# The order of the two token halves in the low-part product of a split float32 projection

## The reference

```python
for i in range(DEPTH):                       # DEPTH = 4
    a = rms_norm(h, norm_mix[i])
    # i % 3 == 0: stick-breaking attention: qkv = a @ w_qkv (1024 x 3072), ..., o @ w_o (1024 x 1024)
    # i % 3 == 1: short gated convolution:  a @ w_in (1024 x 3072), ..., (gate_b * y) @ w_out
    # i % 3 == 2: gated linear attention:   a @ w_in (1024 x 3088), ..., (o * silu(g_out)) @ w_o
    h = h + mixer(a)
    a = rms_norm(h, norm_mlp[i])
    h = h + (relu(a @ w_up) ** 2) @ w_down   # 1024 x 4096 and 4096 x 1024
y = rms_norm(h, norm_final)
```

## Time and profile before

| | |
|---|---|
| median of three runs | 2761.11 us |
| profiled execution, its own time | 2760.71 us |
| its span, first to last instruction | 2759.0 us |
| TensorE busy (matmul) | 2729.8 us, 99% of the span, 20754 matmuls |
| VectorE busy | 1266.0 us, 46% |
| ScalarE busy | 864.6 us, 31% |
| mean busy share of the DMA engines, GB/s | about 2 tenths, 81 GB/s |
| mean granted TensorE clock | 0.995 of full speed |

### The profile page before, as it was taken

The page is one execution under the profiler, slowest core; times in us unless marked ns, Lnnn a source line. Parts: engine busy times, 40 slices in busy tenths (PEclk is TensorE's granted clock), DMA queues, the critical chain, the costliest instruction groups (busy, mean ns, idle before and its releaser), DMA issues.

```text
span 2759.0 us, 48416 instructions
## 1 busy us (share of the span) xinstructions
PE 2729.8 (99%) x20754; PEld 2657.8 (96%) x20754; DVE 1266.0 (46%) x1577; ACT 864.6 (31%) x949; POOL 223.1 (8%) x232
## 2 busy tenths in 40 slices
PE   8999999999999999999999999999999999999998
PEld 8987999999999999999999899999999969999998
DVE  4258433333455434334478543333342494433433
ACT  3147322222312322223224432222331384321222
POOL 4000100000211100000133110000010001000001
PEclk9999999999999999999999999999999999999999
DMA  4211322222222222222212122222222103322221
GB/s 158 78 66 37 115 82 85 83 86 83 77 92 76 79 90 79 90 77 85 84 47 73 44 92 77 91 77 91 77 94 90 47 36 122 96 77 92 77 91 50
DMA packets 205540, 223.64 MB, mean 81 GB/s; under 512 B 3766, under 2 KB 200480, under 8 KB 205392
## 3 DMA queue, kind: packets, MB, share of 16 engines
q1 hardware_dynamic: 200992, 206.06, 23.2%
q0 software_dynamic: 4400, 15.41, 1.6%
HBM read 208.60 MB, written 12.86 MB: 80 GB/s over the span
## 4 chain that ended last, share of the span: by engine, by line
PE 97%; DVE 1%; ACT 1%; issue 0%; DMA 0%; POOL 0%; ACTq 0%; DVEq 0%
PE bank L399 88%; PE bank L511 2%; PE bank L471 1%; PE bank L532 1%; PE bank L703 1%; PE bank L479 0%; PE bank L571 0%; PE bank L651 0%; PE bank L426 0%; PE bank L758 0%; DVE wlo L1195 0%; PE bank L465 0%; DVE e L1300 0%; PE bank L441 0%; PE bank L757 0%
## 5 line engine op out<-in xcount | busy, mean ns | idle before, releaser
L399 PE MATMUL bank<-ahi,whi 128*128 128x288 f32 x3584 | 768.8, 295 | 7.1 <-DVE alo L1220 7.1
L399 PE MATMUL bank<-alo,whi 128*128 128x288 f32 x3584 | 766.2, 294 | 0.0
L399 PE MATMUL bank<-ahi,wlo 128*128 128x288 f32 x3584 | 765.0, 294 | 0.0
L863 ACT ACTIVATE whi<-raw 128x2048 fp32r<-128x2048 f32 x191 | 364.2, 1907 | 829.7 <-PE bank L399 824.0
L399 PEld LDWEIGHTS bank<-ahi,whi 128*128 128x128 f32 x3584 | 574.9, 188 | 11.9 <-DVE wlo L1195 7.2
L399 PEld LDWEIGHTS bank<-ahi,wlo 128*128 128x128 f32 x3584 | 576.0, 188 | 0.0
L399 PEld LDWEIGHTS bank<-alo,whi 128*128 128x128 f32 x3584 | 574.5, 188 | 0.0
L399 PE MATMUL bank<-hhi,whi 128*128 128x288 f32 x2560 | 546.8, 294 | 3.8 <-DVE hlo L1553 2.0
L399 PE MATMUL bank<-hhi,wlo 128*128 128x288 f32 x2560 | 546.1, 294 | 0.0
L399 PE MATMUL bank<-hlo,whi 128*128 128x288 f32 x2528 | 540.9, 294 | 0.0
L1195 DVE TENSOR_TENSOR wlo<-raw,whi 128x2048 fp32r<-128x2048 f32 x192 | 444.1, 2313 | 208.7 <-ACT whi L863 206.1
(11 more groups left out here) (250 smaller groups left out, 1532.0 us busy)
## 6 DMA issues: line engine op xcount, KB each, us to landing
raw<-in_mlp_w_up SPq DMA_DIRECT2D x64, 1024.0 KB, 5.4
raw<-in_mlp_w_down SPq DMA_DIRECT2D x64, 1024.0 KB, 5.1
raw<-in_sb_w_qkv SPq DMA_DIRECT2D x24, 1024.0 KB, 5.2
raw<-in_conv_w_in SPq DMA_DIRECT2D x12, 1024.0 KB, 5.1
raw<-in_gla_w_in SPq DMA_DIRECT2D x12, 1024.0 KB, 5.3
raw<-in_sb_w_o SPq DMA_DIRECT2D x8, 1024.0 KB, 5.2
out<-mixs POOLq DMA_DIRECT2D x2, 2048.0 KB, 7.6
out<-big POOLq DMA_DIRECT2D x2, 2048.0 KB, 8.2
```

The costliest lines, as they stand in the source:

```text
L399: mm = pe.matmul(acc[h][:, 0:HALF], w[:, u, k, m * P:(m + 1) * P], a[:, k, h * HALF:(h + 1) * HALF], start=(k == 0 and w is whi and a is a ...
L863: act.activation(whi[:, 1 - u], raw[:, 1 - u], ACT.Copy).then_inc(w_hi, 1)
```

## The change

In the product of the high weights with the low activations (`w is whi and a is a_lo`) the second token half is computed first, and then the first half. The other two products keep the first half first. So the six matmuls of a slice went to the halves 0, 1, 0, 1, 0, 1, and now go to 0, 1, 1, 0, 0, 1.

```diff
                             for w, a in ((whi, a_hi), (wlo, a_hi)) if low_last else ((whi, a_hi), (whi, a_lo), (wlo, a_hi)):
-                                for h in range(2):
+                                for h in ((1, 0) if w is whi and a is a_lo else (0, 1)):
                                     mm = pe.matmul(acc[h][:, 0:HALF], w[:, u, k, m * P:(m + 1) * P],
                                                    a[:, k, h * HALF:(h + 1) * HALF],
```

## The result

The changed kernel is slower. Its median is 2797.8 us (2797.5 to 2798.3, 4 runs) against 2759.9 us (4 runs of the kernel before). The ratio is 1.0137, with a 95% interval of 1.0125 to 1.0150, or about 37 us. No change was forecast, with a range that ended at 2777 us.

What follows compares the result with a forecast made beforehand. The prediction took TensorE's matmul count times start distance to bound the kernel. Weights, waits and steps at 0 added to 2760.71 us, with the runs' median 0.4 us above, gave 2761 us, range 2753 to 2777 us.

Steps and rivals of the forecast that it cites:

- What bounds the kernel: TensorE, busy 99% of the span; line 399's 18,400 matmuls at 132.2 ns make 2433 us of 2759.0.
- Weights and waits at 0: Line 399: weight loads keep addresses and order, waits and releases stay at the same points; each priced at 0.
- The step from one matmul to the next at 0 ns: Line 399's 6112 same-half steps cost nothing extra; uncertainty 0.5 ns per changed step either way, 3 us.
- The bounds: Limits on the 6112 changed steps of line 399: between 75 us less and 990 us more.
- a toll for changing it: Line 399: bank changes cost up to 12.2 ns per step; full size 2686 us, chance 0.08.
- a stall in it: Line 399: a second matmul accumulating in the same bank waits 162 ns; full size 3751 us, chance 0.03.
- the rhythm of reads and weight loads: Line 399: moving reads and weight loads meet worse, 5 ns per slice once or twice; 2776 to 2792 us, chance 0.09.
- friction between the moving read and the weight load: Line 399: possible source of the unexplained 12.2 ns per step, depending on which addresses meet.
- The signs to look for: Profile checks on line 399: long piece, start distances, means by product, half-clock starts and VectorE's waits.
- The long piece: Unbroken 3072 matmuls of line 399: 406.2 us again, or 2.6 us or twice that longer if the rhythm turns.
- The half-clock stretch: Before 23 us, at half clock, matmul starts should stay 0.24 us apart.
- The sign on VectorE's waits: VectorE's waits for line 399, 471.2, 220.0 and 193.0 us, should keep their sizes in any case but the stall.

Runs made afterwards that it cites:

- banks alone: Kernel before, low product reads halves 0, 1 but writes bank 1 first, then bank 0: 2759.7 us, ratio 0.9998.
- reads alone: Kernel before, low product reads half 1 first but writes bank 0 first, then bank 1: 2796.5 us, ratio 1.0128.
- starts 64 apart: Second half of each product read from token 272: 2763.2 us in the order of the kernel before, 2760.6 us in the changed order.
- second half at 256: Second half of each product read from token 256, not 288, 32 tokens read twice: 2754.0 us in the old order, 2756.3 us in the changed order.
- second half at 224: Kernel before, second half of each product read from token 224, not 288, 64 tokens read twice: 2761.3 us, ratio 1.0003.
- shifted low reads with the order changed: Changed order, low product reading from token 256 for half 1 and token 32 for half 0: 2760.5 us, ratio 0.9999 against the kernel before.
- turn in every product: Kernel before, halves turned around at every product, over the slice boundary too: 2781.9 us, ratio 1.0078.
- low weights in the middle: Kernel before, low weights' product moved to the middle and its halves reversed: 2798.6 us, ratio 1.0137.
- shifted low reads in the old order: Kernel before, low product reading from token 32 for half 0 and token 256 for half 1: 2797.4 us, ratio 1.0136.
- low weights swapped: Kernel before, halves swapped in the low weights' product in place of the low activations': 2792.9 us, ratio 1.0116.

## Why the prediction was wrong

**What bounds the kernel** was right. The time is the number of matmuls times the distance of their starts. Before, that distance is 132.2 ns, now it is 134.4 in the long pieces, and 2.2 ns times the 18,400 matmuls of line 399 would be 40 us; 37 were measured, since some shorter pieces slow down less.

**Weights and waits at 0** fit the trace: the idle time before line 399's high product is 7.0 us (7.1 before), and its weight loads take 188 to 189 ns (188 before).

**The step from one matmul to the next at 0 ns** failed. The sentence that failed is "So the step doesn't ask which operands follow each other. I take 0 ns per step". I had drawn it from line 410 and line 399, which agree at 132.4 and 132.2 ns. But in both of them the halves go 0, 1, 0, 1 without a break, and so do the starts modulo 256 bytes. They differ in which products follow each other and share the one thing that the change alters. The rows of lines 465, 737, 757 and 758 rightly ruled out a part for the bank, as the run with the banks alone showed. They hold no one-pass product of 288 columns, so they could say nothing about the read. The rule of the Trainium skill that the prediction cites ("TensorE: Matmul & The Clock Gate", section "Back-to-back issue gap") has no term for the order and gives 0 as well. The 37 us measured here decide against it.

**The bounds** were set for the bank only: a toll for changing it from below, a stall in it from above. The read had a rival of its own, the rhythm of reads and weight loads, at 0.09. It was the right one in place and sign, since reads alone carry the cost. Its price was mis-sized: 5 ns per slice, once or twice, read from line 680; the runs give 37 us / 3056 = 12 ns. That step was put at 0 and weighs 12 ns per slice. Its reason isn't shown. I had put friction between the moving read and the weight load. The runs show that the starts of the moving reads matter, and that an exchange of high for low weights changes nothing. They don't test the addresses of the weights, so the friction stands as a rival. For it speaks line 680: its starts alternate as in line 399, its weights are others, and its matmuls come 133.5 ns apart in place of 132.2.

**The range** ended at 2777 us, at the smaller of that rival's two prices. The larger, 2792 us, is 6 us under what was measured. So the chance of 0.09 is where the prediction weighed its evidence wrong: it had read in the earlier trace rows that the distance can differ by pattern, and it set that aside for the agreement of rows that all alternate.

**The signs to look for** were useful. The long piece grew, as that rival says, but by 6.8 us and not by 2.6 or 5.2. The means differ by product (299, 295 and 297 ns), as it says too. The half-clock stretch stayed at 0.24 us, as said. The sign on VectorE's waits was wrong, since they grew by 15.2 and 17.2 us without a stall.

What stays open is the rule behind the rates. The pieces of 3072 matmuls of all kernels come at four of them: 404.5, 406.2, 409.6 and 413.0 us, or 131.7, 132.2, 133.3 and 134.4 ns. By the starts modulo 256 bytes within two slices (0 for 0, 1 for 128; the runs with starts 64 apart, at 406.2, are left out):

```text
starts                 long piece   kernels
000000 000000          404.5/406.2  second half at 256, in either order
000000 000000          404.5        cut at 256
000000 000000          406.2        cut at 256 with the order changed
010101 010101          406.2        kernel before, banks alone, second half at 224,
                                    shifted low reads with the order changed
101010 101010          406.2        all reversed
000111 000111          406.2        half outermost
011001 100110          409.6        turn in every product
011001 011001          413.0        changed kernel, reads alone, low weights in the middle,
                                    shifted low reads in the old order
010110 010110          413.0        low weights swapped
```

The sequence doesn't fix the rate by itself. The changed kernel has both 134.4 and 133.3 ns (the piece of 384), the aligned kernels have both 131.7 and 132.2, and line 680 has 133.5 ns with starts that alternate. Why 000111, with four repeats, is free and 011001, with two, isn't, no run here settles. In the half-outermost run the weights go high, high, low twice in a slice, which is a difference that wasn't tried by itself.

## What to carry to other kernels

In a stream of matmuls with no waits, the order in which equal pieces of the moving operand are read can cost over 1%, though no instruction, wait or bank is added. Look at the byte offsets of the pieces: here pieces whose starts differ by multiples of 256 bytes were at least as fast as the kernel before in both orders that were tried, and cutting 576 tokens into 256 and 320 in place of twice 288 gave 0.4%. A row shows that a step is free only for steps that differ in what the change alters, so before pricing an edit at 0 it is worth asking what all the rows at hand have in common.

## What the runs showed of the hardware that was not expected

At full granted clock the distance of the starts takes a few fixed values (131.7, 132.2, 133.3, 134.4 ns for 288 columns), and it holds each of them to 0.02 ns over 3072 matmuls. Changing only the sequence of the moving operand's start addresses modulo 256 bytes moves it from one value to another (406.20 to 412.96 us for 3072, and back), though the sequence alone doesn't say which value a stretch gets: in the changed kernel it is 134.4 ns in most stretches and 133.3 in one. At clock 0.50 the distance is 240 ns in both orders. Two matmuls in a row that accumulate into one PSUM bank run at the same rate as two that change the bank (406.20 us for 3072 in both). Where all starts differ by multiples of 256 bytes and the lengths are equal, one kernel has stretches at 131.7 ns and others at 132.2 ns in the same execution, for the same loop, and its time spreads over 6 us from run to run with the halves in the old order (2750.9 to 2756.6 us) and over 11 us in the changed one.
